# A streamed mixture-of-experts kernel: handing each expert's weights over one step later on the DMA queue

## The reference

```python
def _moe(h, w_router, b_router, w_up, b_up, w_down, b_down):
    logits = (t @ w_router) + b_router             # 512 tokens, 32 experts
    vals, idx = lax.top_k(logits, 4)               # each token picks 4 experts
    gates = jax.nn.softmax(vals)
    ...                                            # rows sorted by expert: xs
    u = xs @ w_up[e] + b_up[e]                     # 1024 -> 512
    glu = jnp.minimum(u[..., ::2], 7.0)
    lin = jnp.clip(u[..., 1::2], -7.0, 7.0)
    a = glu * jax.nn.sigmoid(1.702 * glu) * (lin + 1.0)
    y = a @ w_down[e] + b_down[e]                  # 256 -> 1024
    out = segment_sum(gate * y, token)
```

## Time and profile before

| | |
|---|---|
| median of the runs | 1522.19 us |
| the profiled execution, its own time | 1522.19 us |
| its span, first to last instruction | 1520.4 us |
| granted TensorE clock, mean | 0.933 of 2.4 GHz |
| PE busy | 1327.2 us, 87% |
| DVE, POOL, ACT busy | 642.3, 488.3, 248.2 us |
| DMA, mean rate | 223 GB/s |

### The profile page before, as it was taken

One profiled execution on the slowest core, in us unless ns is written; L12 is line 12 of the kernel. 1 busy time (PEld: TensorE's weight loads), 2 busy tenths in 40 slices (PEclk: granted clock), 3 DMA queues, 4 the chain that ended last, 5 costly groups with the idle time before them and its releaser, 6 DMA issues.

```text
span 1520.4 us, 17770 instructions
## 1 busy us (share of the span) xinstructions
PE 1327.2 (87%) x4216; PEld 684.5 (45%) x4217; DVE 642.3 (42%) x1538; ACT 248.2 (16%) x565; POOL 488.3 (32%) x667
## 2 busy tenths in 40 slices
PE   6886699999999999986996987499999999999965
PEld 2545344444444444434544444344444444444422
DVE  0677125555555222259546757322222222222216
ACT  0111111111111111111113422111111111111111
POOL 0025533334443333323100025333333333333313
PEclk9996799999999999988995988599999999999988
DMA  9963579997897655562135403345746577567434
GB/s 359 366 249 138 225 287 362 349 344 277 332 350 265 237 198 199 172 241 92 61 139 207 186 0 158 111 177 198 274 187 253 211 279 275 196 260 270 158 118 166
DMA packets 92244, 339.22 MB, mean 223 GB/s; under 512 B 17321, under 2 KB 39593, under 8 KB 74674
## 3 DMA queue, kind: packets, MB, share of 16 engines
q1 hardware_dynamic: 50098, 284.23, 49.7%
q0 software_dynamic: 21312, 33.61, 6.0%
q10 hardware_dynamic: 20800, 20.97, 4.0%
HBM read 338.55 MB, written 44.04 MB: 252 GB/s over the span
## 4 chain that ended last, share of the span: by engine, by line
PE 45%; POOL 15%; issue 13%; DVE 13%; POOLq 7%; DMA 4%; ACT 2%; SPq 1%; DVEq 0%; ACTq 0%
PE ps L835 17%; POOL onehot L623 11%; PE ps L808 5%; PE ps L822 4%; PE ps L997 4%; PE ps L797 3%; PE ps L891 3%; PE ps L1055 3%; POOLq L616 2%; POOLq L615 2%; DMA ring<-in_w_ada 2%; DVE big L1498 2%; DMA big<-y_rows 2%; PE ps L714 2%; DVE work L1498 1%
## 5 line engine op out<-in xcount | busy, mean ns | idle before, releaser
L835 PE MATMUL ps<-ring,work 128*128 x576 | 267.1, 607 | 2.1 <-ACT work L1144 2.0
L822 PE MATMUL ps<-ring,work 128*128 x576 | 259.3, 604 | 1.3 <-DVE work L1475 1.3
L822 PE MATMUL ps<-ring,big 128*128 x576 | 253.3, 592 | 0.0
L1479 DVE TENSOR_SCALAR work<-ps 128x256 f32<-128x256 f32 x72 | 30.6, 425 | 403.2 <-PE ps L822 403.2
L623 POOL TENSOR_SCALAR onehot<-cst,rank_now 128x128 bf16<-128x128 f32 x312 | 183.3, 599 | 16.4 <-POOL rank_now L617 16.4
L644 POOL COPY scatter_at<-scatter_ring 128x1 int32 (+1 forms) x72 | 15.0, 208 | 481.6 <-DVE work L1498 245.9
L822 PEld LDWEIGHTS ps<-ring,work 128*128 128x128 f32 x576 | 111.5, 194 | 128.4 <-issue 127.1
L822 PEld LDWEIGHTS ps<-ring,big 128*128 128x128 f32 x576 | 109.2, 190 | 122.6 <-issue 121.2
L835 PEld LDWEIGHTS ps<-ring,work 128*128 128x128 f32 x576 | 104.2, 191 | 111.2 <-issue 107.2
L1140 ACT ACTIVATE work<-work 128x256 f32<-128x256 f32 x72 | 30.0, 417 | 500.0 <-DVE work L1479 500.0
L797 PE MATMUL ps<-vals,onehot 128*128 x312 | 42.5, 176 | 58.2 <-POOL onehot L623 58.0
(11 more groups left out here) (202 smaller groups left out, 1667.8 us busy)
## 6 DMA issues: line engine op xcount, KB each, us to landing
ring<-in_w_up SPq DMA_DIRECT2D x64, 2048.0 KB, 7.8
ring<-in_w_down SPq DMA_DIRECT2D x64, 1024.0 KB, 10.8
ring<-in_w_ada SPq DMA_DIRECT2D x18, 2048.0 KB, 13.9
big<-y_rows SPq DMA_DIRECT2D x8, 2048.0 KB, 7.8
big<-in_w_ada ACTq DMA_DIRECT2D x12, 1024.0 KB, 10.4
big<-in_w_kv_ada ACTq DMA_DIRECT2D x8, 1024.0 KB, 11.9
h_rows<-big SPq DMA_DIRECT2D x8, 512.0 KB, 7.7
ring<-in_w_q SPq DMA_DIRECT2D x2, 2048.0 KB, 10.6
```

Source lines behind the costliest of these rows:

```text
L822: mm = pe.matmul(U, xT[p][:, k, :], ring[:, bass.ds(at + k * UP, UP)], start=False, stop=(k == KC - 1))
L835: mm = pe.matmul(Y[:, h, :], aT[:, k, :], ring[:, bass.ds(at + k * D + h * HALF, HALF)], start=(k == 0), stop=(k == KF - 1))
```

## The change

In `expert_loads` on SP, the hand-over of each expert is put one step later. In step e of the loop, expert e+1 is handed over where it was e+2. The hand-over of expert 1 that stood ahead of the loop is now the first one in it, and behind the loop experts 29, 30 and 31 are handed over where it was 30 and 31.

```diff
                 sp.wait_ge(s["table_ready"], l + 1)
-                pass_on(1, 0)
                 with sp.Fori(0, NE // RING - 1) as turn:
                     for r in range(RING):
 
-                        pass_on((r + 2) % RING, turn + (r + 2) // RING)
+                        pass_on((r + 1) % RING, turn + (r + 1) // RING)
                         e = turn * RING + r
                         end = sp.value_load(table[0:1, bass.ds(e + T_END, 1)], min_val=1, max_val=48)
                         sp.wait_ge(m[l]["down_done"], end)
                         load_expert(l, e + RING, r)
                 for r in range(RING):
-                    if r < RING - 2:
-                        pass_on(r + 2, NE // RING - 1)
+                    if r < RING - 1:
+                        pass_on(r + 1, NE // RING - 1)
                     if r < len(following):
                         load_static(following[r])
```

## The result

The changed kernel takes 1535.59 us (median of 4, 1533.69 to 1536.91) against 1519.99 us before (median of 4, 1515.62 to 1526.88). The ratio is 1.0095, with a 95% interval from 1.0065 to 1.0125. The profiled execution after has a span of 1535.1 us and a mean granted clock of 0.937.

The account below looks back on a forecast made before the run. Bound: two nearly equal paths from the down matmuls to L797, PE's shorter than POOL's. A stall of 1.1 + 0.5 = 1.6 us less 0.6 absorbed, 50 x 1.0 + 1, gave 52 us on 1522.2: 1574 us, range 1551 to 1605.

Parts of the forecast that it names:

- Term 1: On SP, the hand-over at L427 comes after PE's L822 start, by 1.1 us on average.
- term 2: On PE, from SP's semaphore to the first up matmul: 0.5 us, bounds 0 and 0.7.
- Term 4: Number of blocks that stall: 50, after leaving out early hand-overs and experts with two blocks.
- correction for the first two blocks of each loop: No idle time in front of their L797 to absorb the stall, so they lose 0.6 us more each.
- Term 3: Idle time in front of L797 absorbs 0.60 us of each stall, leaving net 1.0 us a block.
- The clock: Rival: the pause before L822 lowers PE's granted clock often, giving between 1594 and 1659 us; chance 0.12.
- Nothing absorbed: Rival: POOL's path moves along with L822, so 50 blocks lose 1.6 us each, 1602 us; chance 0.06.
- Hidden anyway: Rival: PE reaches L822 later than SP's hand-over, so no change, 1522 us; chance 0.05.
- L822 about 1.9 us after the down matmuls: Sign in single-block experts: up matmuls start about 1.9 us after the last L835 ends; 0.28 us in two-block ones.
- Idle time in front of L797 nearly 0: Sign on PE: the idle time ahead of the row matmuls goes to nearly 0.
- A block of 14.0 to 14.4 us: Sign in the expert part: a block takes 14.0 to 14.4 us instead of 13.0 to 13.4.

Follow-up runs that it names:

- experiment 1: POOL builds its onehots before scattering the earlier y tile (POOL's order): 1435.07 us on the kernel before, 1502.77 us on the changed kernel.
- experiment 2: Changed kernel with the hand-over between the next load's two DMA issues: 1519.44 us with the old POOL order, 1472.52 us with POOL's early onehots.
- experiment 3: Changed kernel with more table reads on SP ahead of each hand-over in the loop: 1568.62 us with one read, 1622.44 us with two.
- experiment 5: PE's table read moved earlier in the transposes-first kernel: 1456.94 us; unused read added behind the onehot wait: 1580.55 us in the kernel before, 1438.9 us with early onehots.

## Why the prediction was wrong, step by step

The **bound** was read rightly: two paths from "down matmuls done" to L797, nearly equal, PE's the shorter one.

**Term 1**, the lateness on SP (1.1 us), and **term 2**, from the semaphore to the matmul (0.5 us): right. The mean stall is 1.6 us, as forecast: 67.2 us of idle time in 50 places are 1.34 us each, 0.17 us is the time in which the bias matmul still ran, and 0.1 us the longer run of up matmuls. One reading beside term 1 was wrong: the trace does split the gap from 605.49 to 605.8. SP's loop step (L434, 605.54 to 605.66) and the other wait of the hand-over (L425 at 605.71) lie in it, so it says nothing of how long a semaphore takes.

**Term 4**, 50 blocks: exact. Its correction for the first two blocks of each loop was wrong: they were to lose 0.6 us more because no idle time stands in front of their L797. They gained it back all the same, from 1.54 to 0.92 us up to down in block 3 of the first layer (193.8 before, 198.6 after), with only 0.05 us recorded as idle before.

**Term 3**, what is absorbed, is the step that failed: 0.60 us was taken, and the runs show about 1.3 us (66 us given back in 50 stalls, 1.27 us a block in experiment 1). "The idle time in front of L797 is used up, 0.60 us on average" is right, but the pause had a second part that no row calls idle. While PE's sequencer waits for the onehot it can prepare nothing behind it. The sequencer rows of L797 before, and of L796 after:

```profile
L797 PEldq FUSED_REGOPS  x4: 46/46/51, 612.1 to 612.4; - x4
```

```profile
L796 PEldq FUSED_REGOPS  x4: 46/46/51, 406.6 to 407.0; - x4
```

Before, the four steps ran from 612.1 to 612.4, after the up matmuls had ended at 611.77, and each L797 matmul had to wait for its own, 0.12 us apart; L808 came 0.61 us behind the first. After the change the onehot is ready at the same distance from the down matmuls, but the up matmuls last until 407.57, so the same steps from 406.6 on lie beside them. The saving is the idle 0.60, the 0.51 by which L808 follows sooner, and the 0.16 by which L797 may start before the modelled end of the up matmuls: 1.27. With it the sum is 50 x (1.6 - 1.3) = 15 us, beside 15.6 measured; with differences of this size between two rounded terms the closeness is in part luck, and the table's 14 us against 13.1 is the better test.

It could have been read from the trace before. The row of 181.87 in the earlier trace rows is a block without a pause, and its L797 took 0.24 us, where the rows with a pause say 0.55. Its two neighbours:

```profile
188.83 0.24 PE L797 MATMUL ps<-vals,onehot 128*128 x4
188.94 1.14 PE L808 MATMUL ps<-cst,work 128*128 128x128 f32 x8
```

I used the row of the up matmuls in this block for term 2 and not these for term 3. The row at 200.87 also misled: it has no idle bracket, yet its L797 is 0.55 us long, because the sequencer was just late. A row without idle time is not yet a row without loss.

**The rivals.** The clock did not fall at this stall length; it does from about 2 us on. "Nothing absorbed" is right only where there is no pause to absorb with. "Hidden anyway" was wrong about the change, whose stall is there 50 times, and is right for a stall of 1.0 us. No rival stood where the result fell: between hidden and half absorbed. The range was too narrow below: 1.3 for term 3, which the block at 181.87 shows, gives 1537 us by itself.

**What the after profile was to show.** L822 about 1.9 us after the down matmuls: 1.74 in the block shown, 1.79 on average. Idle time in front of L797 nearly 0: yes, 31.2 us are left in 25 places. Six of them, with 20.1 us, lie ahead of the first block of a layer, and 18 of the other 19 stand behind up matmuls that had no stall. A block of 14.0 to 14.4 us: no, 13.4 on average in both layers, against 13.2 before. A stalled block is 1.79 + 7.13 + 0.92 + 3.60 = 13.4 us, which shows the missing 0.7 us alone.

## What to carry to other kernels

The idle time that a profile books to a wait is not what the wait costs. It can be too little: here 0.60 us was booked and 1.27 came back, because everything that the sequencer must still do behind the wait comes on top, unless queued work covers it. It can be too much: the 37.2 us of experiment 2 cost nothing where another path was later. So price a wait by comparing two blocks, one with it and one without, from one fixed point to the next, and not by its bracket. And where two engines take turns at being late to the same point, delaying the one ahead is free up to the other's full lateness: remove the larger lateness first. Here the order on POOL was worth 84 us, and only behind it does the place of the hand-over cost its full price, 68 us in place of 16.

## What the runs showed of the hardware

- A matmul with an address from a register needs a step of PE's sequencer, one each 0.12 us (L797 from 612.1 to 612.4). A table read with its steps takes 0.65 us on PE (618.73 to 619.38) and 0.50 us on SP (experiment 3). The sequencer was 2.5 us ahead of the array at 602.2, and had lost that lead behind the late waits at 612.1, 618.1 and 400.1. The Trainium skill (Advanced Engine Details and Errata, section "Sequencer Loop") has engine instructions pushed into a queue and control instructions executed by the sequencer itself; the three kernels of experiment 5 agree, with 0.66 us for a read behind a late wait and nothing for one ahead of it.
- The granted clock held at 1.00 through pauses of 1.34 us of mean idle time in the changed kernel, 50 in all. With 1.84 us 8 blocks beyond the first ones had slow matmuls, with 2.34 us 23. In each stall two transposes and one bias matmul went before it and 7 us of dense matmuls followed.
- In the fastest kernel, with its shorter blocks, a side load landed late once and cost PE 9.6 us of idle time. The fastest kernel that was run, 1435.07 us, is the kernel before with POOL's order alone.
